# Neighbourhood attention: the order of VectorE's work between two pairs of heads, and four projection chunks ahead of the first scores

## The reference, cut to what matters

```python
h = rms_norm(x, norm1_g[l]);  z = h @ w_in[l]
a, gate, q, k, v = jnp.split(z, splits, axis=-1)
conv_out = conformer_conv(a, gate, ...)      # u = a * sigmoid(gate); 31 taps; LayerNorm; silu
q = rms_norm(q.reshape(B, S, N_HEADS, HEAD_DIM), q_norm_g[l])   # 8 heads of 64
k = rms_norm(k.reshape(B, S, N_HEADS, HEAD_DIM), k_norm_g[l])
attn_out = neighbourhood_attention(q, k, v, rpb[l])   # each query: 8 x 16 keys around it
mix = jnp.concatenate([conv_out, attn_out], axis=-1)
x = x + mix @ w_out[l]
```

## Time and profile before

| | us |
|---|---|
| median of 3 runs | 2387.98 (2387.67 to 2390.47) |
| the profiled execution | 2388.06 |
| its span | 2386.3 |
| busy PE, DVE, ACT, POOL in the span | 2285.7, 1602.7, 1094.0, 1166.7 |

### The profile page before, as it was taken

How to read it: one execution, slowest core, us unless ns; L and a number is a source line. 1 busy time by engine, 2 the same in 40 slices (tenths; PEclk the granted TensorE clock), 3 DMA queues, 4 the chain that set the end, 5 groups by cost and what they waited for, 6 DMA issues and landing times. The chain is left out here.

```text
span 2386.3 us, 28947 instructions
## 1 busy us (share of the span) xinstructions
PE 2285.7 (96%) x10276; PEld 1756.2 (74%) x10276; DVE 1602.7 (67%) x1909; ACT 1094.0 (46%) x1776; POOL 1166.7 (49%) x832
## 2 busy tenths in 40 slices
PE   8988988989999999999999998996999999999999
PEld 6866655867888887888765565574788888888887
DVE  7889885486666567547856667639766655444587
ACT  5156656254444443222236666526666652222342
POOL 1000000469777877877521121142877777777732
PEclk9999998999999999999999999998999999999999
DMA  3211100413435338883200000212556677976412
GB/s 131 66 33 33 35 19 11 192 54 115 176 121 188 134 149 322 327 320 139 95 27 18 19 27 5 97 71 88 238 238 239 253 295 306 374 277 247 146 39 80
DMA packets 89165, 342.90 MB, mean 144 GB/s; under 512 B 22400, under 2 KB 23168, under 8 KB 76096
## 3 DMA queue, kind: packets, MB, share of 16 engines
q1 hardware_dynamic: 88368, 336.65, 37.5%
q10 hardware_dynamic: 656, 4.41, 0.5%
HBM read 224.16 MB, written 116.27 MB: 143 GB/s over the span
## 5 line engine op out<-in xcount | busy, mean ns | idle before, releaser
L1124 PE MATMUL ps<-operand,turn_weights 128*128 128x512 f32 x3192 | 735.6, 392 | 17.6 <-POOL turn_weights L730 5.5
L1124 PEld LDWEIGHTS ps<-operand,turn_weights 128*128 128x128 f32 x3192 | 599.3, 188 | 152.5 <-issue 15.2
L730 POOL TENSOR_TENSOR turn_weights<-turn_raw,turn_weights 128x512 fp32r<-128x512 f32 (+1 forms) x330 | 444.6, 1358 | 226.4 <-ACT turn_weights L1586 225.8
L1124 PE MATMUL ps<-hidden_operand,turn_weights 128*128 128x512 f32 x2268 | 517.5, 390 | 3.4 <-issue 1.4
L1124 PEld LDWEIGHTS ps<-hidden_operand,turn_weights 128*128 128x128 f32 x2268 | 424.8, 188 | 95.8 <-issue 6.0
L2803 DVE TENSOR_TENSOR branch_out<-ps,branch_out 128x1024 f32<-128x1024 f32 x172 | 210.5, 1224 | 201.3 <-PE ps L1124 200.3
L1586 ACT ACTIVATE turn_weights<-turn_raw 128x512 fp32r<-128x512 f32 (+1 forms) x330 | 204.9, 624 | 266.7 <-PE ps L1124 251.3
L690 POOL TENSOR_TENSOR weight_hi<-weight_raw,zero_col 128x1024 fp32r<-128x1024 f32 (+1 forms) x26 | 54.0, 2077 | 546.7 <-PE ps L1023 376.0
L844 PE MATMUL ps<-input_hi,weight_hi 128*128 128x512 f32 x592 | 197.0, 414 | 22.9 <-DVE input_lo L2368 9.8
L844 PE MATMUL ps<-input_lo,weight_hi 128*128 128x512 f32 x656 | 206.2, 396 | 0.0
L844 PE MATMUL ps<-input_hi,weight_lo 128*128 128x512 f32 x592 | 184.9, 394 | 0.0
(11 more groups left out here) (351 smaller groups left out, 3559.4 us busy)
## 6 DMA issues: line engine op xcount, KB each, us to landing
hidden_operand<-hidden_kept SPq DMA_DIRECT2D x91, 1024.0 KB, 8.0
hidden_kept<-hidden_parts SPq DMA_DIRECT2D x54, 1024.0 KB, 8.7
hidden_kept<-hidden_parts SPq DMA_DIRECT2D x27, 1536.0 KB, 6.2
turn_raw<-w_ff SPq DMA_DIRECT2D x40, 512.0 KB, 4.1
turn_raw<-w_mlp SPq DMA_DIRECT2D x32, 512.0 KB, 4.3
turn_raw<-w_mlpd SPq DMA_DIRECT2D x32, 512.0 KB, 4.4
turn_raw<-w_ffd SPq DMA_DIRECT2D x20, 512.0 KB, 4.6
weight_raw<-w_out SPq DMA_DIRECT2D x16, 512.0 KB, 3.7
```

Of the source, the lines that this page charges most:

```text
L730: pool_.tensor_tensor(place(p, 1), place(p, 1, WT) if raw is None else raw, bits(place(p, 0)), ALU.subtract).then_inc(s["st_lo"], 1)
L1124: ins = mm(PS[:, b, :], weights(p, w, k), tokens(p, a, k), start=(FRESH[p] and k == 0 and step == 0), stop=(k == n - 1 and step == 2), ski ...
```

## The change

Three things are moved, nothing is added or taken away.

On PE, chunks 2 and 3 of the second pair's q unit are issued ahead of `scores(0)`. Chunk 2 stood between `scores(0)` and `scores(1)`, chunk 3 in slot 0 of block 0.

On DVE, in every pair change: the taps at j = 4, 5 and 6 are shared out again, so that two taps stand ahead of `head_norm(4c + 6)` and one ahead of `head_norm(4c + 7)`; `head_lo(c + 1, 1)`, k's low part, stands directly behind q's; and `evac(c + 1, 2, 0)`, v's, stands directly behind that, still at j = 6 and ahead of one tap more, where it used to open j = 7. The total of 124 taps is the same.

```diff
--- before.py
+++ after.py
@@ -1043,10 +1043,9 @@
                     for i in range(3):
                         out_half(0, j - 6, MIX_ORDER[i])
 
-            for what in (0, 1):
+            for what in (0, 1, 2, 3):
                 next_piece(0, what)
             scores(0)
-            next_piece(0, 2)
             scores(1)
             v_turn(0, 0)
             for c in range(4):
@@ -1056,7 +1055,8 @@
                     def slot(i):
                         if j < 7 and c < 3:
                             for what in BESIDE[j][i]:
-                                next_piece(c, what)
+                                if n or what > 3:
+                                    next_piece(c, what)
                         elif j == 7 and c < 2:
                             for what in BESIDE[j][i]:
                                 next_piece(c + 1, what)
@@ -2522,10 +2522,14 @@
                     evac(c + 1, 1, 0)
                     conv(1)
                 elif j == 5:
+                    conv(2)
                     head_norm(4 * c + 6, 5)
                 elif j == 6:
+                    conv(1)
                     head_norm(4 * c + 7, 5)
                     head_lo(c + 1, 0)
+                    head_lo(c + 1, 1)
+                    evac(c + 1, 2, 0)
 
             def second_part(c, j):
                 if j == 1:
@@ -2535,11 +2539,9 @@
                     weight_lo(U_QKV + 3 * c + 5)
                 elif j == 5:
                     weight_lo(U_QKV + 3 * c + 6)
-                conv((3 if c else 4, 2, 1, 2, 3, 3, 2)[j])
+                conv((3 if c else 4, 2, 1, 2, 2, 2, 1)[j])
                 if j == 3:
                     head_norm(4 * c + 5, 5)
-                elif j == 6:
-                    head_lo(c + 1, 1)
 
             def last_pair(j):
                 if j == 0:
@@ -2569,7 +2571,6 @@
                 for j in range(CBLOCKS):
                     n = CBLOCKS * c + j
                     if j == CBLOCKS - 1 and c < 3:
-                        evac(c + 1, 2, 0)
                         conv(1)
                         scores_in(n + 1, 0)
                         scores_in(n + 1, 1)
```

## The result

The changed kernel took 2377.19 us (median of 5 runs, 2375.41 to 2379.88) beside 2389.59 us for the kernel before (5 runs, 2387.67 to 2391.81): a ratio of 0.9949, with an interval of 0.9938 to 0.996. That is 12.4 us between the medians, 9.6 to 14.8 us by the interval. The forecast was 2376.5 us, and 11.5 us less. (The record before the prediction had three of the five runs of the kernel before, with a median of 2387.98.)

A forecast was written before the change was run, and what follows sets the result against it. The prediction took DVE's work plus its waits to bound the attention stage. It summed 0.86 + 2.5 + 3.8 + 4.6, less three times 0.1, to 11.5 us, giving 2376.5 us (2374.7 to 2378.5; 8 in 10: 2373.7 to 2381.2).

The forecast's parts named there:

- What bounds the stage: Attention stage: DVE's work plus its waits set the length; 12.1 us of waits in the three pair-change stretches.
- The start, 0.86 us: First pair's second scores: DVE's 0.86 us wait goes with two chunks issued earlier; bounds nothing to 1.0 us.
- The first norm wait: First pair change, ahead of k's first norm: one more tap covers the wait for guess_squared, so 0.73 us go.
- the norm of the second change: Second pair change: of the 2.31 us norm wait, 1.0 to 1.1 stays if PE's clock falls there again.
- k_lo and evac directly behind q_lo: Pair changes on DVE: at most 0.1 us wait per pair for k_hi, and 1.4 us slack for PE's chunk 23.
- Rival (e): Slower: lower clock on chunks 18 to 23 makes DVE wait behind chunk 23, 17 us in three pairs, 2394; chance 0.03.
- The pair changes, 2.5, 3.8 and 4.6 us less 0.1 each: Savings up to the next pair's second scores at the three pair changes, less 0.1 us each for k_hi.
- Rival (a): The lower PE clock stays in the pair changes: only 8.7 us saved, 2379.3 us; chance 0.21.
- The total: Whole kernel: 11.5 us less, 2388.0 to 2376.5 us, with everything from the fourth pair's second scores moving as a block.
- The signs: Profile: score waits within 1 us, PE holes under 1.5, clock above 0.95, fourth pair's second scores near 341.3 us.
- Weighing a rule: PE clock: activity judged on a free-running schedule, so equal idle time may or may not be charged after a shift.
- Rivals (c) and (d): Half kept through new DVE waits, 2381 to 2382.5 us, 0.10; all waited for again at output projection, 2387 to 2388, 0.04.

The follow-up runs named there:

- e1: The kernel before with only PE's edit (chunks 2 and 3 ahead of the first scores): 2389.32 us, ratio 1.0000 to before.
- e2: The changed kernel with PE's order taken back to the old one, all DVE edits kept: 2377.70 us, ratio 0.9954 to before.
- e11: e5 plus six unused matmuls in PE's hole before chunk 0 or the first mean part, at three pair changes: 2381.77 us, ratio 0.9962 to before.
- e4: The kernel before with only k_lo and v's evac moved directly behind q_lo, taps ahead of the norms unchanged: 2382.00 us, ratio 0.9972 to before.
- e5: The changed kernel with only v's evac taken back to j = 7, behind one tap: 2387.51 us, ratio 0.9992 to before.
- changed_again: The changed kernel run once more, nothing altered: 2378.30 us, ratio 0.9957 to the kernel before.

## Why the prediction was right, step by step

- **What bounds the stage**: right. DVE's work plus its waits gave each stretch to about 0.1 us (23.37, 24.53 and 23.83 us measured; 23.4, 24.5 and 23.95 by the terms and the earlier trace rows). Its 12.1 us of waits were read from busy time; the waits in brackets are 2.13, 4.53 and 4.29, 10.95 in all. The stretches shrank by 10.74 with 9.75 of them gone, and the rest is the shorter listed busy time and smaller gaps between instructions. Between the pair changes nothing moved (39.57 us before, 39.53 and 39.54 after).
- **The start, 0.86 us**: wrong. It was gained at 148.91 and lost at block 4; from the first k_lo to the taps of the first pair change it is 49.14 us before and 49.33 after. My lower bound of zero named the mechanism (PE's clock falls once more and PE is late behind it), and the runs show it: behind the hole ahead of chunk 8 PE needed 5.97 us to block 4's scores and not 4.83. The value I took was wrong, because I looked at the present wait and not at what ends the next ones. e1 gives 0.0 by its median (2 us either way), e2 without it the whole gain by its median, and the mean over ten profiles is 0.2 us at block 4.
- **The first norm wait and the norm of the second change**: right. 0.73 went, and 1.20 stayed of 2.31 where I said 1.0 to 1.1.
- **k_lo and evac directly behind q_lo**: right. q_lo to k_lo is 1.21 us, 0.07 over a bare step of 1.14, and chunk 23 was never waited for. Rival (e), which lived on that slack, did not show up in any run.
- **The pair changes, 2.5, 3.8 and 4.6 us less 0.1 each**: 2.44, 3.68 and 4.62 measured. The larger values came because the clock stayed up, which I had tied to the shrinking hole. That tie is only partly shown: e11 shows that filling a hole keeps the clock up, but in e4 it fell behind a hole of 1.12 us in the second change and not behind 1.11 in the third, so the length of the hole alone does not decide. Rival (a) is refuted for this kernel by a granted clock of 1.00, 0.96 and 1.00, but e5 shows that it was near: with one tap between k_lo and the evac the clock falls in all three changes, and the gain on the kernel before is 1.9 us, not the 8.7 of rival (a).
- **The total**: the stage gave 10.6 us where I had 11.5, the fourth pair 1.9 more in the profiled pair of runs. I had said that the fourth pair moves as a block. It didn't: 1.7 of its 1.9 us are the clock's at L1004, which fell there before and stayed up after, as it did and didn't in other kernels (38.0 in e2 and e4, 39.8 in e1 and e5). So the hit on 12.4 is partly luck; the interval of 9.6 to 14.8 holds both.
- **The signs**: those on waits, holes and clock came true (no wait for second scores, holes of 0.51 to 0.97 us, a clock of 0.96 or more). The fourth pair's second scores are read at 343.49 us and not near 341.3; 1.24 us of the difference stand ahead of the first k_lo, and the other 0.95 are about the start's lost term.
- **Weighing a rule**: that equal holes are charged or not after a shift is what the runs show: the same hole of 1.6 us ahead of chunk 16, v's first, left the clock up in the changed kernel's first and third pair and cost a norm wait of 1.20 us in its second, and changed_again had none there, but waited 0.63 and 1.36 us at block 4 of its third pair.
- **Rivals (c) and (d)**: no new waits for exponentials or means came up. Nothing was waited for again behind the stage: the rest is 3.0 us longer in the profile of the changed kernel, but 1993.3 in changed_again, beside 1993.6 before.

## What to carry to other kernels

Where two engines hand one buffer back and forth, the release of the buffer (here the evac of the one PSUM place) deserves a place directly behind the work that lets the other engine start, before any filler. In this kernel one filler instruction of 1.3 us between them made the stage 8.5 us longer over three places, more than half of it by TensorE's clock. An edit that fills a hole early in a chain may be worth nothing in the end, so look up what ends the next waits, not how long the present one is. When TensorE has a short hole ahead of a critical burst, filling it with matmuls that nobody needs is a test of the clock. Here it also gave 5.7 us against e5, but the changed kernel, without any such filler, is another 3.5 us faster beside it (2378.30 and 2381.77). And before a difference of 2 us between two profiles is explained by a change, compare the granted clock in the places that the change doesn't touch.

## What the runs showed of the hardware that I had not expected

Two holes, of 0.49 or about 0.97 us and of 1.42 to 1.51 us, with 1.0 us of small matmuls between them, stood at the fall of the granted clock from its 2.4 to its 1.2 GHz level in all three pair changes of e5 (steps start 0.85 us apart and not 0.46). With the second hole filled it stayed up in all three. Single holes of 0.51 and 0.97 us ahead of the first scores, in the changed kernel, did not cost it, while one of 1.12 us in e4 did. Equal holes did not do the same each time: e4's third change had one of 1.11 us and kept the clock, 1.6 us ahead of chunk 16 cost it in one pair of three, and behind the same 2.97 us ahead of chunk 8 PE needed between 4.83 and 6.03 us for the same work. The two lengths of the part behind the stage (1993 and 1996 us), and those of the fourth pair (38 and 39.8), come in the main from one such fall each. What decides whether a given hole costs the clock is left open by these runs.
